# Moving the convolution branch's LayerNorm into the attention loop, starting attention two places later, and taking PSUM banks in rotation

## The reference, cut to what matters

```python
p, g_lin = jnp.split(z_b, 2, axis=-1)
c = p * jax.nn.sigmoid(g_lin)
c = causal_depthwise_conv(c, cv_w[l], cv_b[l])
c = jax.nn.silu(layer_norm(c, cv_ln_g[l], cv_ln_b[l]))
y_b = c @ w_b_out[l]
...
z = jnp.einsum("bhqd,bhkd->bhqk", q_blk, k[:, :, :ctx]).astype(jnp.float32) * scale
log_1m_beta = jnp.where(mask, jax.nn.log_sigmoid(-z), 0.0)
cs = lax.cumsum(log_1m_beta, axis=3)
log_a = jax.nn.log_sigmoid(z) + (cs[..., -1:] - cs)
a = jnp.where(mask, jnp.exp(log_a), 0.0)
outs.append(jnp.einsum("bhqk,bhkd->bhqd", a.astype(v.dtype), v[:, :, :ctx]))
...
gates = jax.nn.sigmoid(z_g.reshape(bsz, t, N_BRANCH, d) + b_gate[l].astype(z_g.dtype))
merged = gates[:, :, 0] * y_a + gates[:, :, 1] * y_b + gates[:, :, 2] * y_c
```

## Time and profile before

| | us |
|---|---|
| median of 3 runs | 2217.44 |
| lowest, highest | 2216.53, 2217.89 |
| the profiled execution: time | 2216.53 |
| its span, first to last instruction | 2214.7 |
| PE busy | 2168.6 |
| DVE, POOL, ACT busy | 1187.4, 920.3, 897.1 |
| PE, 1529 to 1741 us (the loop's first two branches and the run-up) | 195.99 of 212 |

### The profile page before, as it was taken

One profiled execution on the slowest core, in us unless ns is written; L12 is line 12 of the kernel. 1 busy time (PEld: TensorE's weight loads), 2 busy tenths in 40 slices (PEclk: granted clock), 3 DMA queues, 4 the chain that ended last, 5 costly groups with the idle time before them and its releaser, 6 DMA issues.

```text
span 2214.7 us, 25698 instructions
## 1 busy us (share of the span) xinstructions
PE 2168.6 (98%) x10002; PEld 1796.3 (81%) x10002; DVE 1187.4 (54%) x1835; ACT 897.1 (41%) x1306; POOL 920.3 (42%) x438
## 2 busy tenths in 40 slices
PE   8989999999999999999999999999899999999999
PEld 6877888888888888888888888887778788888887
DVE  6883476353345343465763524997456423765351
ACT  5554444232333333344442424434567434443231
POOL 2423444444443343434444444644322454444443
PEclk9999999999999999999999999999999999999999
DMA  3201223222322222222223224321111242323232
GB/s 131 67 20 59 90 94 103 97 95 98 110 93 81 91 86 81 89 84 86 95 95 105 89 92 159 105 77 67 67 58 58 86 133 88 104 97 101 90 105 95
DMA packets 57657, 200.43 MB, mean 90 GB/s; under 512 B 6400, under 2 KB 7168, under 8 KB 57280
## 3 DMA queue, kind: packets, MB, share of 16 engines
q1 hardware_dynamic: 57536, 198.79, 26.8%
HBM read 194.30 MB, written 4.19 MB: 90 GB/s over the span
## 4 chain that ended last, share of the span: by engine, by line
PE 88%; DVE 7%; ACT 3%; issue 1%; DMA 0%; SPq 0%; POOL 0%; DVEq 0%; ACTq 0%; POOLq 0%
PE ps L314 27%; PE ps L316 26%; PE ps L315 26%; DVE ps L1993 2%; PE ps L342 2%; PE ps L344 2%; PE ps L343 2%; PE ps L357 1%; PE ps L1136 1%; PE ps L1723 1%; PE ps L388 1%; ACT WH L285 0%; DMA WS<-in_w 0%; DVE SC L1351 0%; DVE SM L1349 0%
## 5 line engine op out<-in xcount | busy, mean ns | idle before, releaser
L295 POOL TENSOR_TENSOR WL<-WS,WH 128x1024 fp32r<-128x1024 f32 (+2 forms) x362 | 855.4, 2364 | 1191.3 <-ACT WH L285 1191.3
L314 PE MATMUL ps<-H,WH 128*128 128x512 f32 (+1 forms) x1776 | 700.3, 394 | 8.8 <-DVE H L472 8.8
L316 PE MATMUL ps<-H,WL 128*128 128x512 f32 (+1 forms) x1776 | 694.7, 391 | 0.0
L315 PE MATMUL ps<-H,WH 128*128 128x512 f32 (+1 forms) x1776 | 694.4, 391 | 0.0
L285 ACT ACTIVATE WH<-WS 128x1024 fp32r<-128x1024 f32 (+2 forms) x362 | 374.6, 1037 | 441.0 <-PE ps L316 343.6
L314 PEld LDWEIGHTS ps<-H,WH 128*128 128x128 f32 (+1 forms) x1776 | 335.2, 189 | 81.0 <-POOL WL L295 8.3
L316 PEld LDWEIGHTS ps<-H,WL 128*128 128x128 f32 (+1 forms) x1776 | 334.5, 188 | 72.0 <-issue 0.8
L315 PEld LDWEIGHTS ps<-H,WH 128*128 128x128 f32 (+1 forms) x1776 | 335.1, 189 | 67.6 <-issue 0.6
L314 PE MATMUL ps<-G,WH 128*128 128x512 f32 x880 | 343.2, 390 | 1.5 <-DVE G L1445 1.5
L315 PE MATMUL ps<-G,WH 128*128 128x512 f32 x880 | 342.4, 389 | 0.0
L316 PE MATMUL ps<-G,WL 128*128 128x512 f32 x880 | 342.4, 389 | 0.0
(11 more groups left out here) (234 smaller groups left out, 2026.5 us busy)
## 6 DMA issues: line engine op xcount, KB each, us to landing
WS<-in_w SPq DMA_DIRECT2D x337, 512.0 KB, 3.2
WS<-in_w SPq DMA_DIRECT2D x24, 384.0 KB, 3.0
X<-in_x SPq DMA_DIRECT2D x8, 256.0 KB, 5.3
xs<-X SPq DMA_DIRECT2D x1, 2048.0 KB, 9.4
X<-xs SPq DMA_DIRECT2D x8, 256.0 KB, 4.7
out<-X SPq DMA_DIRECT2D x8, 256.0 KB, 2.8
X<-in_sg SPq DMA_DIRECT2D x1, 1344.0 KB, 5.6
SC<-in_rot SPq DMA_DIRECT2D x4, 256.0 KB, 3.6
```

Of the source, the lines that this page charges most:

```text
L295: e.tensor_tensor(lo, raw, hi.bitcast(F), ALU.subtract).then_inc(*P.sig("w_lo", i))
L314: e.matmul(out, lh, rh, start=start, stop=False)
L315: e.matmul(out, lh, rl, start=False, stop=False)
L316: return e.matmul(out, ll, rh, start=False, stop=stop)
```

## The change

Four things change, all in the gated block.

- The attention's first step moves from place 4 to place 6 (`C_FIRST` 3 to 5). The 35 steps end at place 46 where they ended at 45. Before, of the last two places of each pair (6k+4 and 6k+5), both hold a step in pairs 0 to 3, and one is empty in pairs 4 (29), 5 (35) and 6 (40). After it, one is empty in pair 1 (11), both hold a step in pairs 2 to 6, and the empty places are 0 to 5, 11, 18, 25, 32, 39, 45 and 47.
- The LayerNorm of the convolution moves from ahead of the loop into it. PE: `mean` after place 2, `deviation` after place 8, the spread after place 12. DVE: `centre` 3, `sums` 5, `dve_rstd` 9, `normed` 12. ACT: `squares` 4, `act_root` 9, `silus` 16.
- POOL's low parts of the SiLU output move from pair 0 to pair 2.
- `P.longest_free` is not set any more: banks are taken in rotation inside the loop too.

```diff
-C_FIRST = 3
+C_FIRST = 5
...
-    mean()
...
-    deviation()
     pair(1)
...
-    P.longest_free = True
     slots, place = iter(C_SLOT), [0]
-
-    def last_rows():
-        pair(2)
-        spread_mm(P, e, "cn", 1, 0)
-    early = {0: last_rows, 1: lambda: pair(3)}
+    early = {0: lambda: pair(2), 1: lambda: pair(3), 2: mean, 8: deviation, 12: lambda: spread_mm(P, e, "cn", 1, 0)}
...
-    P.longest_free = False
...
     cast(("cv", 2))
-    squares()
     pair(0)
...
-    act_root(P, e, "cn", 1)
...
-    early = {1: silus}
+    early = {4: squares, 9: lambda: act_root(P, e, "cn", 1), 16: silus}
...
-    centre()
-    sums()
     pair(0)
...
-    dve_rstd(P, e, "cn", 1, 512, 0)
     pair(2)
-    normed()
     pair(3)
...
+    early = {3: centre, 5: sums, 9: lambda: dve_rstd(P, e, "cn", 1, 512, 0), 12: normed}
...
+        if place[0] in early:
+            early[place[0]]()
+        place[0] += 1
...
-            if (bi, mp) == (0, 0):
+            if (bi, mp) == (0, 2):
```

More of the change, by code:

```diff
@@ L1667, in pe_gated, with pair @@
             stat(m - 1)
+    toks = tokens(P, e, "cv", [("cv", u) for u in range(4)])
+    next(toks)
+    stat(7)
+    drop(P, ("cst", "sum"))
+    next(toks)
+    rows_mm(P, e, "cst", 16)
+    next(toks)
+    def pair(i):
+        for m in C_PAIRS[2 * i:2 * i + 2]:
+            if m == 0:
+                e.wait_ge(*P.at("halves"))
+            half_spread_mm(P, e, "cst", 2 * m, c_halves(P), [c_rows(P, lo) for lo in range(2)])
+    pair(0)
+    next(toks)
+    next(toks, None)
+    pair(1)
     def mean():
@@ L1677, in deviation @@
         stat_mm(P, e, "cn", 1, 0, P.m["ACC"][:, :], ("acc", ("cn", 3)), first=True)
[L1679 to L1684, removed]
-    mean()
[L1686 to L1695, removed]
-    deviation()
-    pair(1)
     def logits(n):
@@ L1868, in pair @@
             e.activation(c_qq(P, m, 0) if m < 4 else c_kk(P, m - 4, 0), P.X(m), ACT.Copy).then_inc(*P.sig("cq_hi", m))
+    cast(("cv", 2))
+    pair(0)
+    cast(("cv", 3))
+    for j in range(4):
+        e.wait_ge(*P.at("tok", ("cv", 3, j)))
+        e.activation(c_vv(P, j, 0), P.ps(("cv", j)), ACT.Identity, scale=P.root(j)).then_inc(*P.sig("vv_hi", j))
+    pair(1)
+    cast(("gate", 0, 0))
+    pair(2)
+    pair(3)
     def squares():
@@ L1875, in squares @@
                 act_square(P, e, ("cn", k), P.sc(k * T), ("c_centred", k))
-    cast(("cv", 2))
-    squares()
[L1878 to L1883, removed]
-    act_root(P, e, "cn", 1)
-    cast(("gate", 0, 0))
-    pair(2)
-    pair(3)
     def silus():
@@ L2090, in pair @@
             P.end["ps", ("cst", "spread", 2 * m)] = ("cq_n", m)
+    pair(0)
+    for j in range(4):
+        e.wait_ge(*P.at("vv_hi", j))
+        e.scalar_tensor_tensor(c_vv(P, j, 1), P.ps(("cv", j)), P.root(j), c_vv(P, j, 0).bitcast(F), ALU.mult,
+                               ALU.subtract).then_inc(*P.sig("vv_lo", j))
+        P.end["ps", ("cv", j)] = ("vv_lo", j)
+    for i in range(1, 4):
+        pair(i)
     def centre():
@@ L2164, in attend @@
                 P.end["ps", ("pv", (pr, hd))] = ("o_split", (pr, hd))
-    slots = iter(C_SLOT)
+    slots, place = iter(C_SLOT), [0]
     def slot(bi):
```

## The result

The changed kernel takes 2232.22 us (median of 4 runs, 2231.72 to 2234.85) where the kernel before takes 2216.99 us beside it (4 runs, 2215.75 to 2217.89): ratio 1.0072, 95% interval [1.0054, 1.0089]. It is slower by 15.2 us. The profiled execution took 2230.88 us.

What follows compares the result with a forecast made beforehand. PE bounds the kernel, busy 2168.6 of 2214.7 us. In the touched stretch, losses were to rise from 24.2 to 39.9 us, 15.7 more: 2217.4 + 15.7 = 2233 us, own range 2223 to 2242, range for all 2218 to 2246.

Steps and rivals of the forecast that it cites:

- place 10, bank; clock: PE waits 4.3 us at place 10 for ACT's exponential to free a reused bank, with 3.2 us of lower clock.
- place 17, split; bank behind the SiLUs; clock: At place 17 PE waits 1.9 us for DVE's split, 6.2 for item 8's bank, and loses 3.3 to clock.
- place 29, split; bank; clock: At place 29 PE waits 1.6 us for the split; bank reuse was listed but given no cost, nor was clock.
- left over: 2.0 us of small waits as before and 0.7 us for banks at places 19 and 37.
- What is removed: Gone: spread's wait 2.2 us plus 1.7 clock, first steps' waits 1.8 and 1.7, place 11's 3.31 plus 3.1 clock.
- The bank waits: In rotation a bank can return at once; PE waits for its last exponential, from none to 4.3 us each.
- The SiLUs at place 16: SiLUs between two attention steps delay ACT's exponential; PE waits 6.2 us at place 17, bounds nothing to 11.
- The clock behind a wait: PE's granted clock falls after longer waits, as in the earlier trace: 3.4 us lost behind a 4.15 us wait.
- The later start: First-step waits and place 11's go, but pairs with both last places full rise from three to five.
- rivals 1 and 2: Bank waits cost nothing, 2215 us (0.10); or slack makes banks and newly full pairs 5 and 6 free, 2204 us (0.06).
- Rival 3: Clock does not recover between waits at places 10, 13, 15, 17: 12 us added, 2245 us; chance 0.10.
- The table load: By the skill's 2.66 us per change, three added loads cost 4.1 us more, 2237 us; the prediction used 1.28 per load.

## Why the prediction was right, point by point

The time, 2232.22, was forecast as 2233, inside the range. What the change adds came from the causes named, of what it removes one cause was another (below), and the close hit of the sum is in part luck. The sizes, in us of waiting and of clock:

| step of the prediction | forecast | measured |
|---|---|---|
| place 10, bank; clock | 4.3; 3.2 | 4.34; 1.4 |
| place 13, scores' bank | 1.7 | 2.31 |
| place 15, bank | 1.1 | 0.98 |
| place 17, split; bank behind the SiLUs; clock | 1.9; 6.2; 3.3 | 1.83; 6.12; 2.4 |
| place 23, split | 1.5 | 1.66 |
| place 29, split; bank; clock | 1.6; 0; 0 | 2.64; 1.18; 3.1 |
| place 34, bank; clock | 4.3; 3.4 | 3.29; 1.2 |
| place 35, bank | 0.6 | 0.69 |
| place 41, split and bank; clock | 2.4; 1.7 | 0.83 + 1.40; 1.7 |
| left over | 2.7 | 0.37 + 0.98 |

The waits add up to 28.3 forecast and 28.6 measured, the clock to 11.6 and 9.7. The clock's entries are those of one profile. In the second profile of the changed kernel place 10 lost 2.1 and place 41 nothing, so that the agreement at place 41 is luck.

- **What is removed** was right as a sum: 2.2, 1.8, 1.7 and 3.31 us went. The experiment with empty places confirmed the cause of the 3.31 and 4.15. The 2.2 went with the move of the LayerNorm, which no run made alone. For the 1.8 and 1.7 the prediction named ScalarE's work alone. The runs show that VectorE's low parts beside GpSimd belong to it: ahead of the 1.7 one of them took 2.44 us where it takes 0.28 with GpSimd idle.
- **The bank waits** were right in place and nearly in size, and the run without the rotation shows that with their clock they are the whole difference: 2232.2 against 2216.7 us. Working the lag from a place with the same widths was good to 0.2 us at places 10 and 15, to 0.6 at 13 and to 1.0 at 34. The reuse at place 29 was listed and priced at nothing; that was 1.18 us and, with the split's wait of 2.64 just ahead, the clock's 3.1. This is the one term that was clearly missed. Clock losses 4.9 us smaller than forecast at 10, 17 and 34 made up for it in this profile; that the two errors cancel is luck.
- **The SiLUs at place 16**, the term with the widest bounds (0 to 11), came to 6.12 against 6.2. But the attribution needs care: it was booked to the SiLUs' move, while the runs show that it takes both. Without the rotation it is nothing in this order of steps; in the order before, where places 17 and 18 both hold a step, it is a wait of 7.26 us for the split instead. Likewise the root's load is 1.5 us of place 10's wait, and moving it elsewhere gained nothing.
- **The clock behind a wait** was taken from the earlier trace rows as if the chip gave the same each time. The low level lasted on after the waits, but where the wait is long, as at place 17, part of it runs out while PE stands still: PE was busy for 5.88 of 12 us there. So 6.12 us of waiting lost 2.4, less than the 3.4 behind 4.15 us before.
- **The later start** came out even by its ratio (1.0009), as removed and newly full places had it, and **rivals 1 and 2** fell with the waits on the exponential. Rival 3, a clock that stays low, was not seen in the changed kernel: it is back at 1.00 by 1577, 1621, 1679, 1705 and 1737 us, at most some 10 us behind a wait.
- **Which bank.** The prediction let the rotation cost through the banks of scores alone. On the kernel before, the rotation by itself costs nearly as much, mostly through the banks of head outputs. The loss came in both orders tried, and does not hang on where the scores fell in this one; that was not foreseen.
- **The table load.** The Trainium skill ("ScalarE: Activation LUTs", section "What ACT_TABLE_LOAD costs") puts a change of set at about 2.66 us. The changed kernel does not agree: the SiLUs' load began at 1607.18, 0.02 us behind the end of the operation before it, and the first SiLU at 1608.48, 1.30 us later.

## What to carry to other kernels

A bank is free for its next writer only when its last reader is done, and that reader may stand on a slow chain; so the order in which banks are handed out is a wait in the engine that must never wait. Look in the program's order for reuse within a few matmuls, and price each by that reader's lag at a like place. Where two steps lie closer together than the chain between them takes, leave a place empty between them: that made this kernel 0.49% faster, and with a later start 0.65%, though what the start adds is not clear of noise. And where an operation is slower than its like elsewhere, look at what the engine beside it did: three of the waits here hung on that.

## What the hardware showed that was not expected

- The granted clock is no fixed answer to a wait: behind the same 2.30 us it was 0.65 over 4 us in one profile and 1.00 in three others, and behind the spread's 2.2 us it was 0.50, 0.63 and four times 1.00. So a clock loss read from one profile is good to a few us at most, and a change of some us in it alone is not shown to be the effect of an edit. Such a loss can also hide in a wait: behind 1.88 us it made PE 1.6 us later at the next one, which shrank from 1.72 to 0.17.
- VectorE's operations with all operands in SBUF stretch to the length of GpSimd's beside them: 0.35 to 1.42 us and 0.56 to 1.50 us beside low parts of 1.4 us each. Beside a subtraction of 2.4 us one took 2.44 instead of 0.28. Moving GpSimd's work by one weight subtraction took away 2.6 us of waiting and 2.7 of low clock. The Trainium skill ("SBUF — State Buffer", section "SBUF: two separate sides") says that a VectorE operation with two inputs in SBUF and a GpSimd operation that reads SBUF don't share their ports: the one that comes second waits until the other has ended. The trace agrees in size for the operations with two inputs: they are stretched to about the length of GpSimd's (1.50 beside 1.4, 2.44 beside 2.4). Of the cast, which has one input and went from 0.35 to 1.42, this says nothing.
